# A forgetting attention rebuilt by pairs of heads: scores in halves of the systolic array, the gate as a product of its own, values as weights, output born transposed

## The reference

```python
FOX_HEADS = 16
FOX_HD = 64
FOX_QBLOCK = 128
...
for blk in range(t_len // FOX_QBLOCK):
    s0 = blk * FOX_QBLOCK
    e = s0 + FOX_QBLOCK
    s = jnp.einsum("bhqd,bhkd->bhqk", q[:, :, s0:e], k[:, :, :e]).astype(jnp.float32) * scale
    s = s + log_f_cum[:, :, s0:e, None] - log_f_cum[:, :, None, :e]
    mask = (s0 + jnp.arange(FOX_QBLOCK))[:, None] >= jnp.arange(e)[None, :]
    p = jax.nn.softmax(jnp.where(mask, s, -jnp.inf), axis=-1)
    outs.append(jnp.einsum("bhqk,bhkd->bhqd", p.astype(v.dtype), v[:, :, :e]))
o = jnp.concatenate(outs, axis=2)
return o.transpose(0, 2, 1, 3).reshape(b_sz, t_len, FOX_WIDTH) @ w_o
```

## Time and profile before

| what | value |
|---|---|
| runs | 1712.9, 1715.28 and 2855.63 us; median 1715.28 us |
| profiled execution | span 1715.1 us (no time of its own is given beside the span) |
| TensorE busy | 1690.7 us, 99% of the span |
| VectorE, ScalarE, GpSimd busy | 609.9, 655.8 and 671.5 us (36%, 38%, 39%) |
| mean granted TensorE clock | 0.997 of full speed |
| DMA | 145.06 MB, mean 85 GB/s |

### The profile page before, as it was taken

How to read it: one execution, slowest core, us unless ns; L and a number is a source line. 1 busy time by engine, 2 the same in 40 slices (tenths; PEclk the granted TensorE clock), 3 DMA queues, 4 the chain that set the end, 5 groups by cost and what they waited for, 6 DMA issues and landing times.

```text
span 1715.1 us, 23484 instructions
## 1 busy us (share of the span) xinstructions
PE 1690.7 (99%) x9318; PEld 1427.2 (83%) x9318; DVE 609.9 (36%) x1196; ACT 655.8 (38%) x1012; POOL 671.5 (39%) x522
## 2 busy tenths in 40 slices
PE   6999999999999999999999999999999999999999
PEld 6787889898888888887888898888888887887887
DVE  3459325430100011523156240100001445788661
ACT  4654524442222222523354342222222545554651
POOL 3533333334444455443410334444455433453002
PEclk9999899999999999999999999999999999999999
DMA  5212110422222322322220122222322232222001
GB/s 196 74 70 79 51 61 18 169 76 92 90 100 96 110 98 98 116 84 97 76 75 2 48 71 102 98 98 98 126 99 96 82 118 99 74 76 96 26 2 50
DMA packets 23491, 145.06 MB, mean 85 GB/s; under 512 B 3536, under 2 KB 4304, under 8 KB 7408
## 3 DMA queue, kind: packets, MB, share of 16 engines
q1 hardware_dynamic: 23408, 143.90, 23.8%
HBM read 141.72 MB, written 2.10 MB: 84 GB/s over the span
## 4 chain that ended last, share of the span: by engine, by line
PE 69%; issue 13%; POOL 10%; DVE 5%; ACT 2%; DMA 1%; POOLq 0%; SPq 0%; ACTq 0%; DVEq 0%
POOL wlo L2623 10%; PE PS L453 5%; PE PS L454 5%; PE PS L452 5%; PE PS L485 4%; PE PS L343 4%; PE PS L346 4%; PE PS L338 4%; PE PS L486 4%; PE PS L487 4%; PE PS L1642 3%; PE PS L1609 3%; PE PS L961 2%; PE PS L1631 2%; PE PS L466 2%
## 5 line engine op out<-in xcount | busy, mean ns | idle before, releaser
L2623 POOL TENSOR_TENSOR wlo<-wraw,whi 128x512 fp32r<-128x512 f32 (+1 forms) x476 | 625.9, 1346 | 996.2 <-ACT whi L145 996.2
L145 ACT ACTIVATE whi<-wraw 128x2048 fp32r<-128x2048 f32 (+1 forms) x119 | 225.6, 1896 | 240.5 <-PE PS L346 184.1
L452 PE MATMUL PS<-hT_hi,whi 128*128 128x512 f32 x704 | 274.1, 389 | 0.0
L453 PE MATMUL PS<-hT_lo,whi 128*128 128x512 f32 x704 | 273.9, 389 | 0.0
L454 PE MATMUL PS<-hT_hi,wlo 128*128 128x512 f32 x704 | 273.9, 389 | 0.0
L1544 DVE TENSOR_TENSOR act_sb<-sil,PS 128x512 f32 x44 | 30.2, 687 | 428.6 <-ACT sil L1519 428.6
L1519 ACT ACTIVATE sil<-PS 128x512 f32<-128x512 f32 x44 | 26.4, 599 | 355.4 <-PE PS L454 335.5
L452 PEld LDWEIGHTS PS<-hT_hi,whi 128*128 128x128 f32 x704 | 132.2, 188 | 27.5
L453 PEld LDWEIGHTS PS<-hT_lo,whi 128*128 128x128 f32 x704 | 132.2, 188 | 27.5
L454 PEld LDWEIGHTS PS<-hT_hi,wlo 128*128 128x128 f32 x704 | 132.1, 188 | 27.2
L485 PE MATMUL PS<-whi,hT_hi 128*128 128x512 f32 (+2 forms) x288 | 112.3, 390 | 0.1
(11 more groups left out here) (401 smaller groups left out, 3109.8 us busy)
## 6 DMA issues: line engine op xcount, KB each, us to landing
wraw<-wpack SPq DMA_DIRECT2D x125, 1024.0 KB, 4.9
gain<-gains SPq DMA_DIRECT2D x10, 512.0 KB, 6.5
x_sb<-x SPq DMA_DIRECT2D x8, 512.0 KB, 5.7
out<-x_sb SPq DMA_DIRECT2D x3, 512.0 KB, 2.8
csb<-consts SPq DMA_DIRECT2D x1, 704.0 KB, 13.5
out<-x_sb SPq DMA_DIRECT2D x2, 256.0 KB, 2.1
vh<-vecs SPq DMA_DIRECT2D x1, 96.0 KB, 6.4
small<-vecs SPq DMA_DIRECT2D x1, 80.0 KB, 11.9
```

Of the source, the lines that this page charges most:

```text
L145: act.activation((whi[q % 2] if static is not None else hi_of_slot(n))[:, w], wraw[q % 2][:, w], ACT.Copy).then_inc(w_hi, 1)
L452: nc.tensor.matmul(o, whi[q][w], hT_hi[:, k, :], start=(k == 0), stop=False)
L453: nc.tensor.matmul(o, whi[q][w], hT_lo[:, k, :], start=False, stop=False)
L2623: p.tensor_tensor(lo[:, a:b], wraw[q][:, a:b], hi[:, a:b].bitcast(F32), ALU.subtract).then_inc(w_lo, 1)
```

## The change

Heads are handled as pairs. Queries and keys of two heads stay in the 128 partitions in which the projection leaves them (`Q2`, `K2`), head 2p in the lower 64 and head 2p+1 in the upper 64. A step ("macro") is one pair and one query block; the order within a pair is i = 0, 3, 1, 2, and all four blocks of a pair come before the next pair.

- Scores: one f32 product per head over 64 rows, each head in its half of the array's rows and with its own PSUM bank.
- Gate: the part that depends on the query falls out of the softmax, and only the row of the keys is added. It is held as high and low fp32r parts in `c2`, and one single-pass product per head, with a column of a selection matrix repeated 128 times as weights, adds it to the scores. No DMA is needed.
- Copies of the turned probabilities: one instruction for both heads (`copy_views`), by VectorE for i = 1 and 2 (128x512 and 128x768) and by ScalarE for i = 0 and 3 (128x256 and 128x1024).
- Values: V is the weights (128 rows, 64 columns) and the turned probabilities stream; the two heads write the lower and upper 64 partitions of one bank, so the output stands transposed.
- Sums: the 1/sum must now lie along the free axis. GpSimd spreads the eight row sums of a pair over 128x512 values (`pool_rows`), TensorE turns them (`pe_sums`, 4 transposes), VectorE inverts all 128x512 (`dve_inverse`) and multiplies (`dve_final`). ScalarE rounds the result into `hT_hi` and GpSimd makes `hT_lo`. The `Turn` of the output is gone (its 32 transposes are as many as those of the sums).
- The output projection starts within the last two steps with query blocks 1 and 3.

The diff, cut to its core:

```diff
-        KA = at("KA", AT_ARENA, [P, FH, SEQ])
-        QA = at("QA", AT_ARENA + 32 * KB, [P, FH, SEQ])
+        FP = FH // 2
+        K2 = at("K2", AT_ARENA, [P, FP, SEQ])
+        Q2 = at("Q2", AT_ARENA + 16 * KB, [P, FP, SEQ])
+        fp = [at(f"fp{i}", AT_ARENA + 32 * KB + 4 * KB * i, [P, 2, SEQ]) for i in range(2)]
+        fo_t = [at(f"fo_t{i}", AT_ARENA + 40 * KB + 2 * KB * i, [P, SEQ]) for i in range(2)]
+        c2 = at("c2", AT_ARENA + 44 * KB, [P, SEQ], F32R)
+        sel = at("sel", AT_ARENA + 46 * KB, [P, FH], F32R)
...
+            ORDER = (0, 3, 1, 2)
...
+            def pe_scores(self, m):
+                t = nc.tensor
+                p, i = self.macros[m]
+                if m >= 2:
+                    t.wait_ge(sem("fx_exp"), 2 * (m - 2) + 2)
+                for r in range(2):
+                    x = slice(64 * r, 64 * r + 64)
+                    t.matmul(self.score(m, r), Q2[x, p, i * P:(i + 1) * P], K2[x, p, 0:(i + 1) * P], start=True, stop=False)
+                for r in range(2):
+                    x = slice(64 * r, 64 * r + 64)
+                    t.matmul(self.score(m, r), sel[x, 2 * p + r:2 * p + r + 1].to_broadcast([64, P]), c2[x, 0:(i + 1) * P],
+                             start=False, stop=True).then_inc(sem("fx_score"), 1)
+
+            def pe_turn(self, m):
+                t = nc.tensor
+                i = self.macros[m][1]
+                if m >= 1:
+                    t.wait_ge(sem("fx_pt"), m)
+                for r in range(2):
+                    t.wait_ge(sem("fx_exp"), 2 * m + r + 1)
+                    for j in range(i + 1):
+                        last = t.transpose(PS[:, self.turned[r], j * P:(j + 1) * P], fp[m % 2][:, r, j * P:(j + 1) * P], ident)
+                last.then_inc(sem("fx_turned"), 1)
+
+            def pe_values(self, m):
+                t = nc.tensor
+                p, i = self.macros[m]
+                t.wait_ge(sem("fx_pt"), m + 1)
+                if m % 4 == 0 and p >= 1:
+                    t.wait_ge(sem("fx_inv"), p)
+                for j in range(i + 1):
+                    for r in range(2):
+                        last = t.matmul(PS[64 * r:64 * r + 64, self.outs[p % 2], i * P:(i + 1) * P], FV[:, j, (2 * p + r) * FD:(2 * p + r + 1) * FD],
+                                        fpt[m % 2][:, r, j * P:(j + 1) * P], start=(j == 0), stop=(j == i))
+                last.then_inc(sem("fx_pv"), 1)
+
+            def pe_sums(self, p):
+                t = nc.tensor
+                t.wait_ge(sem("fx_rows"), p + 1)
+                if p:
+                    t.wait_ge(sem("fx_final"), p)
+                for i in range(TT):
+                    last = t.transpose(PS[:, self.outs[(p + 1) % 2], i * P:(i + 1) * P], frs[:, i, :, :].rearrange("p r d -> p (r d)"), ident)
+                last.then_inc(sem("fx_sums"), 1)
+
+            def pe(self, begun, hooks):
+                for m in range(self.n + 2):
+                    if begun <= m < self.n:
+                        self.pe_scores(m)
+                    if m in hooks:
+                        hooks[m]()
+                    if m % 4 == 1 and m > 4:
+                        self.pe_sums(m // 4 - 1)
+                    if 0 <= m - 1 < self.n:
+                        self.pe_turn(m - 1)
+                    if 0 <= m - 2 < self.n:
+                        self.pe_values(m - 2)
...
+            def copy_ready(self, eng, m):
+                eng.wait_ge(sem("fx_turned"), m + 1)
+                if m >= 2:
+                    eng.wait_ge(sem("fx_pv"), m - 1)
+
+            def copy_views(self, m):
+                w = (self.macros[m][1] + 1) * P
+                return fpt[m % 2][:, :, 0:w], PS[:, self.turned[0]:self.turned[0] + 2, 0:w]
+
+            def by_vector(self, m):
+                return self.macros[m][1] in (1, 2)
+
+            def act_high(self, p):
+                a = nc.scalar
+                a.wait_ge(sem("fx_final"), p + 1)
+                a.activation(hT_hi[:, p, :], fo_t[p % 2][:, :], ACT.Copy).then_inc(sem("fx_hi"), 1)
+
...
+            def dve_inverse(self, p):
+                v = nc.vector
+                v.wait_ge(sem("fx_sums"), p + 1)
+                v.reciprocal(fri[:, :], PS[:, self.outs[(p + 1) % 2], :]).then_inc(sem("fx_inv"), 1)
+
+            def dve_final(self, p):
+                v = nc.vector
+                v.wait_ge(sem("fx_inv"), p + 1)
+                v.wait_ge(sem("fx_pv"), 4 * p + 4)
+                if p >= 2:
+                    v.wait_ge(sem("fx_lo"), p - 1)
+                v.tensor_tensor(fo_t[p % 2][:, :], PS[:, self.outs[p % 2], :], fri[:, :], ALU.mult).then_inc(sem("fx_final"), 1)
+
+            def dve(self, begun):
+                v = nc.vector
+                for m in range(self.n + 1):
+                    if begun <= m < self.n:
+                        self.dve_max(m)
+                    if m >= 1 and self.by_vector(m - 1):
+                        self.copy_ready(v, m - 1)
+                        o, i = self.copy_views(m - 1)
+                        v.tensor_copy(o, i).then_inc(sem("fx_pt"), 1)
+                    if m % 4 == 1 and m > 4:
+                        self.dve_inverse(m // 4 - 1)
+                    if m % 4 == 2 and m > 4:
+                        self.dve_final(m // 4 - 1)
+                self.dve_inverse(FP - 1)
+                self.dve_final(FP - 1)
...
+            def pool_rows(self, p):
+                e = nc.gpsimd
+                e.wait_ge(sem("fx_exp"), 8 * p + 8)
+                if p:
+                    e.wait_ge(sem("fx_sums"), p)
+                e.tensor_copy(frs.rearrange("p i r d -> p (i r) d"), bt(self.rs[:, 8 * p:8 * p + 8], [P, 8, FD])).then_inc(sem("fx_rows"), 1)
+
+            def pool_low(self, p):
+                e = nc.gpsimd
+                e.wait_ge(sem("fx_hi"), p + 1)
+                e.tensor_tensor(hT_lo[:, p, :], fo_t[p % 2][:, :], hT_hi[:, p, :].bitcast(F32), ALU.subtract).then_inc(sem("fx_lo"), 1)
+        FIRST = Pairs(((2, 3), (6, 7)), (4, 5), (0, 1))
...
-            a.activation(crow[0][:, :], PS[0:16, 5, :], ACT.Copy).then_inc(sem("c_rows"), 1)
-            a.activation(crow[1][:, :], PS[0:16, 5, :], ACT.Copy, scale=-1.0).then_inc(sem("c_rows"), 1)
+            a.wait_ge(sem("c_zero"), 1)
+            a.activation(c2[0:FH, :], PS[0:FH, 5, :], ACT.Copy, scale=-1.0).then_inc(sem("c_high"), 1)
+            a.wait_ge(sem("c_low"), 1)
+            a.activation(c2[64:64 + 48, :], c2[0:48, :].bitcast(F32), ACT.Copy).then_inc(sem("c_both"), 1)
...
+            def first_tile(tt, n):
+                t.wait_ge(sem("fx_exp"), n)
+                slot(0, [tt], False)
+
+            n = FIRST.n
+            FIRST.pe(2, {2: last_heads, n: lambda: first_tile(1, 2 * n - 2), n + 1: lambda: first_tile(3, 2 * n)})
+            slot(1, [1], False)
+            t.wait_ge(sem("fx_pt"), n)
             slot(0, [2], False)
-            turn.tile_done(nc.tensor, 1)
-            turn.pe_tile(3)
-            slot(0, [1], False)
-            turn.pe_tile(0)
-            slot(0, [3, 0], True)
-            slot(1, range(TT))
-            mix.pe_last(lambda m, tiles: slot(2 + m, tiles), after)
+            t.wait_ge(sem("fx_final"), FP)
+            slot(0, [0], True)
+            slot(1, [3, 2, 0], True)
+            FO.pe_last(lambda m, tiles: slot(2 + m, tiles), NF1.T)
```

More of the change, by code:

```diff
@@ L1766, in pe_heads @@
+        FIRST = Pairs(((2, 3), (6, 7)), (4, 5), (0, 1))
         def pe_heads(stage, start=None):
             b = BASE[stage]
-            h0 = 8 if stage == "fq" else 0
+            h0 = 4 if stage == "fq" else 0
             for m in range(2, 4):
-                nc.tensor.wait_ge(sem("heads_a"), h0 + 2 * (m - 1))
-                nc.tensor.wait_ge(sem("heads_v"), h0 + 2 * (m - 1))
+                nc.tensor.wait_ge(sem("heads_a"), h0 + m - 1)
+                nc.tensor.wait_ge(sem("heads_v"), h0 + m - 1)
@@ L1777, in act_heads @@
                 nc.scalar.wait_ge(w_used, b + m + 1)
[L1778 to L1780 removed]
+                nc.scalar.activation(dst[:, 2 * m, :], PS[:, 2 * ((b + m) % 2), :], ACT.Copy,
+                                     scale=scale).then_inc(sem("heads_a"), 1)
                 act_split(b + m + 2)
@@ L1786, in dve_heads @@
                 nc.vector.wait_ge(w_used, b + m + 1)
[L1787 to L1789 removed]
+                nc.vector.tensor_scalar(dst[:, 2 * m + 1, :], PS[:, 2 * ((b + m) % 2) + 1, :],
+                                        scale, None, ALU.mult).then_inc(sem("heads_v"), 1)
         def pe_fox_scores():
[L1793 to L1797 removed]
+            nc.tensor.wait_ge(sem("heads_a"), 7)
+            nc.tensor.wait_ge(sem("heads_v"), 7)
+            nc.tensor.wait_ge(sem("sel"), 4)
+            nc.tensor.wait_ge(sem("c_both"), 1)
+            for m in range(2):
+                FIRST.pe_scores(m)
         def pe_foxproj():
@@ L1892, in dve_foxproj @@
             v.tensor_tensor(lf[:, :, :], fm[:, :, :], fln[:, :, :], ALU.subtract).then_inc(sem("lf"), 1)
```

(41 more changed lines are left out.)

115 lines of the change are left out of this document (68 added, 47 removed).

## The result

The changed kernel takes 1723.3 us (median of 5 runs, 1720.3 to 1724.6) against 1715.7 us before: ratio 1.0041, 95% interval 1.0030 to 1.0052. The forecast was 1722 us, range 1706 to 1731, with 97% on "within 2%". It is slower by 7.6 us, a little more than the 6.7 us forecast. The profiled run has a span of 1721.5 us and a time of 1723.35 us.

What follows compares the result with a forecast made beforehand. TensorE's issue was taken to bound the attention before; with the change, a 12.4 us round containing VectorE's wide reciprocal. Start 17.8, six rounds 74.4 and the end made 148.2 us against 141.6, hence 1722 us, range 1706 to 1731.

Steps and rivals of the forecast that it cites:

- Score and value passes in halves: TensorE's score and value products: both array halves run at once, 2.27 us and 2.2 us per pair.
- The two rivals in which halves don't overlap: TensorE: column halves one after the other, 1734 us, 10%; row halves overlapping by only one pass, 1727 us, 5%.
- Gate: TensorE's added fp32r products, one pass per head, both halves at once: 0.63 us per pair.
- Changes of shape: TensorE's array switching between scores, transposes and values: about 0.17 us each, 12 per pair, 2.0 us.
- TensorE's whole list: Scores, gate, transposes, values and shape changes per pair: 9.7 us, against 10.8 + 0.44 before.
- VectorE: Its work per pair: maxima 4.0, copies 1.65, scaling 0.69, wide reciprocal 3.4, together 9.8 us, as full as TensorE.
- The rival at 4.3 us: VectorE's wide reciprocal costs more, 4.3 us instead of about 3.4, giving 1728 us; chance 13%.
- The round: One pair in program order, from one reciprocal to the next: 12.4 us, against 10.8 before.
- The start of the stage: From first scores to first reciprocal: 7.4 us plus 10.4 us of laid out steps, 17.8 us.
- The end: After the last but one reciprocal: 7.7 us to the first output product, then output projection, last slot and closing transposes.
- The sum: Stage from start, six rounds and end: 148.2 us against 141.6, so 6.6 us more.
- The cheap reciprocal: VectorE's wide reciprocal takes up to some 1.2 us, TensorE stays the bound at 10.1 us a round: 1706 us, 15%.

Runs made afterwards that it cites:

- values head by head: The narrow version with each step's value products ordered all of head 0, then all of head 1, instead of alternating: 1712.1 us.
- narrow version: The changed kernel with VectorE inverting a pair's eight row sums (128x8) before GpSimd spreads them, a plain copy replacing the wide reciprocal: 1706.7 us.
- the split moved: One weight split on ScalarE moved from before the first copy to behind the sixth step: 1721.7 us in the changed kernel, 1706.5 us in the narrow version.
- doubled kernel: The changed kernel with the wide reciprocal done twice per pair, the first into a spare tile: 1755.7 us.
- version from a copy: The changed kernel with ScalarE copying the turned sums out of PSUM and VectorE taking the one wide reciprocal from that copy: 1743.0 us.
- narrow without gate: The narrow version without the gate's products, so its scores lack the key's forget-gate term: 1703.1 us.

## Why the prediction was right

- **Score and value passes in halves.** Forecast: two heads at a time, 2.3 and 2.2 us a pair. Shown: passes of two heads start 6 to 7 ns apart (885.317 and 885.323 for scores, 887.573 and .580 for values), and the 16 value passes of block 3 last until the next scores 895.34 - 894.32 = 1.02 us, eight pairs at 0.109 and a change of shape. The two rivals in which halves don't overlap fall.
- **Gate.** 0.63 us a pair forecast, at least 0.47 by the run without it.
- **Changes of shape.** 0.17 us each forecast. Two transposes and the change behind them take 899.31 - 899.00 = 0.31, so 0.09 over 0.22, and the first pass after a change is 0.05 longer than the next (0.160 against 0.109 by the starts of the values head by head): 0.145. The Trainium skill, "TensorEngine Tiling (Array Packing)", section "Key Properties", says that a change of mode drains the array, without a number; the 0.145 us fit that, though the trace doesn't show what they are spent on. TensorE's whole list was put at 9.7 us a pair; in the narrow version it is busy for 39.04 of 40 us, 9.6 of each round of 9.86.
- **VectorE.** 9.8 us a pair forecast. By the records: eight maxima 4.10, copies 0.96 and 0.69, scaling 0.69, reciprocal 3.35, together 9.8. The reciprocal's extrapolation from 16 and 32 columns held over sixteen times the width: (3352 - 352) / 480 = 6.25 ns per column. The rival at 4.3 us falls.
- **The round.** 12.4 us forecast, 11.90 measured. In the order of the forecast's list: reciprocal 3.27 (3.40), two maxima, exponential and hand-overs 1.41 (1.48), ScalarE's copy and back 1.07 (1.19), transposes 0.59 (0.58), values of block 3 1.02 (1.11), scores of block 0 0.49 (0.54), transposes of block 2 0.80 (0.80), values of block 1 0.59 (0.66), scores and gate of block 3 1.39 (1.23), maxima 1.27 (1.40). Each step is there; most were costed 0.05 to 0.13 us dear, the last scores 0.16 cheap. Six rounds: 3.0 us less than forecast.
- **The start of the stage.** 17.8 us forecast up to the first reciprocal, 876.08 - 855.62 = 20.5 measured. This step failed in two ways. The layout left out the weight split on ScalarE before the first copy, which made TensorE wait for 2.0 us; and it had no term for the clock, which was 0.77 from 865 to 870 and 0.89 from 870 to 875. Three runs part the two: 17.1 us (873.51 - 856.41) with the split moved, 18.9 (873.24 - 854.34) in the narrow version, which has the same gap of 2.00 us and no half clock behind it, and 20.5 here. So the gap is worth 1.8 us and the clock 1.6. That shows in the stage's length of profiled runs, not clearly in the time. The narrow version's rows:

```profile
864.71 1.06 PE L1799 MATMUL PS<-csb,fp 128*128 128x128 f32 x8 [2.00 <-ACT fpt L1873]
```

```profile
865.00:870.00 5.00, 5.00 (x51) 3.56 (x48) 2.35 (x10) 2.94 (x9) 4.22 (x4) 1.00 0.02 3
```

- **The end.** 56.0 us forecast, 1004.85 - 947.49 = 57.4 measured, with the clock at 0.80 and 0.86 between 950 and 960. With the split moved the clock was 1.00 there and the end took 1002.35 - 946.44 = 55.9; so the 1.4 us are the clock's.
- **The sum.** 6.6 us more forecast for the stage: -3.0 +2.7 +1.4 makes 7.7, and 7.6 was measured. The errors nearly cancel: some 3 us of the 7.6 are half clock (1.6 at the start, 1.4 at the end) that no term of the forecast had, and they stand against rounds that were costed dear. The mechanism was right; that the number fits to 1 us is luck.
- **The cheap reciprocal.** The rival gave 1706 us, TensorE as the bound again, up to some 1.2 us of reciprocal. The narrow version is that case: 1706.7 us, round 9.86 where 10.1 was laid out. With a round that grows one for one above that, the point is 3.35 - (11.90 - 9.86) = 1.3 us.

The loss is thus one instruction per pair. The change does give back time on TensorE, 9 us as the narrow version shows, and with the wide reciprocal the kernel is 16.6 us slower than that.

## What to carry to other kernels

A long instruction on an engine with room to spare by its busy share can set the time, if other engines' next step stands behind it in its list. It costs nothing until it is the longest way through the round (here up to some 1.3 us of 3.35) and its whole further length from there on. Lay out one round in order before counting shares. Take reciprocals on the few columns that are distinct, and spread the result, not the other way round. If a copy is moved to another engine to free one, ask who then stands still for it.

## What was not expected of the hardware

- Two array halves run side by side even when their products are not neighbours in the list: the second half began past three waiting products of the first, and not past four or more.
- Half clock came with waiting of TensorE, but the length of a gap doesn't tell whether it comes. It came in every steady round of the doubled kernel (0.50 for 6.8 us, behind waits of 4.32 us), and in five of the six steady rounds of the version from a copy (0.78 to 0.89 over the round), though the sixth, at 1.00, had the same waits of 0.73 and 2.98 us. In the change the gaps of 1.11 and 0.80 us left the rounds from 876 to 947 at 1.00, and the same two gaps at 951 and 953 stood before and in a stretch of 0.50 (953.0 to 956.4). Of eight kernels with a gap of 2.0 or 2.1 us at the start, five were at half clock soon behind it or in its last part, and three (narrow, narrow without gate, doubled) were not. What decides is open. The lower clock made two kernels dearer than the waits alone: the doubled one by 1.5 us a round (the mean round of 16.7 less 11.9 and 3.35).
- A reciprocal costs 6.25 ns per column from 16 to 512 columns, six times a maximum's, from PSUM and from SBUF alike (3352 and 3353 ns).
